# Per-head modulation product moved to GpSimd and VectorE block turns of k and v, in a fused DeltaNet, attention and FFN layer

## The reference, cut to what matters

```python
m = silu(cond) @ w_ada + b_ada        # -> shift1, scale1, gate1, shift2, scale2, gate2
h = rmsnorm(x) * (1 + scale1) + shift1
u = h @ w_in                          # q,k,v,z of 8 DeltaNet heads, betas, attention q,k,v, gates
# A: per head (8 heads, width 128): short conv + silu on q,k,v, l2norm, chunked gated delta
#    rule forward and backward:  v_new = T^-1 (v*beta) - w S ;  o = q S + A v_new ;
#    S = S*gl + (k*decay)^T v_new
# B: neighbourhood attention
x = x + gate1 * ((sig(gA) * (oA @ w_pa) + sig(gB) * (oB @ w_pb)) @ w_out)
x = x + gate2 * swiglu(rmsnorm(x) * (1 + scale2) + shift2)
```

## Time and profile before

| | us |
|---|---|
| median of three runs | 1302.97 (1302.94 to 1303.77) |
| profiled execution | 1302.37 |
| its span, first to last instruction | 1300.6 |

### The profile page before, as it was taken

How to read it: one execution, slowest core, us unless ns; L and a number is a source line. 1 busy time by engine, 2 the same in 40 slices (tenths; PEclk the granted TensorE clock), 3 DMA queues, 4 the chain that set the end, 5 groups by cost and what they waited for, 6 DMA issues and landing times.

```text
span 1300.6 us, 26090 instructions
## 1 busy us (share of the span) xinstructions
PE 1284.3 (99%) x9814; PEld 1212.4 (93%) x9814; DVE 962.6 (74%) x2396; ACT 701.2 (54%) x1578; POOL 172.8 (13%) x161
## 2 busy tenths in 40 slices
PE   7999999999999999999999999999999999999998
PEld 6898999999999999999988889999999999999998
DVE  6677867667686867767456666668999698987995
ACT  5564746465564746465366664347564355634643
POOL 1002020202001020200302320000103300041022
PEclk9999999999999999999999999999999999999999
DMA  9743543434243334325335216431323323233313
GB/s 313 242 131 96 166 122 100 118 94 118 55 142 90 116 103 120 89 72 153 115 113 169 77 51 207 124 82 33 98 67 97 98 70 93 66 100 96 83 57 106
DMA packets 207715, 144.51 MB, mean 111 GB/s; under 512 B 9455, under 2 KB 197015, under 8 KB 207463
## 3 DMA queue, kind: packets, MB, share of 16 engines
q1 hardware_dynamic: 207303, 142.72, 37.4%
q10 hardware_dynamic: 288, 0.13, 0.0%
HBM read 126.67 MB, written 17.99 MB: 111 GB/s over the span
## 4 chain that ended last, share of the span: by engine, by line
PE 92%; DVE 3%; SPq 2%; ACT 1%; issue 1%; DMA 1%; DVEq 0%; ACTq 0%
PE ps L1311 32%; PE ps L1957 25%; PE ps L1700 7%; PE ps L1615 3%; PE ps L1841 2%; PE ps L1937 2%; PE ps L1553 2%; PE ps L1622 2%; SPq L931 2%; PE ps L1439 1%; PE ps L1634 1%; PE ps L1809 1%; PE ps L1285 1%; PE ps L1795 1%; PE ps L1916 1%; PE ps L1693 1%
## 5 line engine op out<-in xcount | busy, mean ns | idle before, releaser
L1311 PE MATMUL ps<-hT_r,WAH_r 128*128 128x320 f32 x624 | 154.9, 329 | 0.5
L1311 PE MATMUL ps<-xT_r,WAH_r 128*128 128x320 f32 x624 | 142.0, 309 | 0.0
L1957 PE MATMUL ps<-d_part_r,W_r 128*128 128x320 f32 x660 | 136.7, 310 | 1.1 <-DVE xT L3388 0.7
L1311 PE MATMUL ps<-hT_r,W_r 128*128 128x320 f32 x588 | 132.6, 308 | 0.0
L1311 PEld LDWEIGHTS ps<-hT_r,WAH_r 128*128 128x128 f32 x624 | 100.3, 189 | 10.8 <-issue 9.8
L1957 PEld LDWEIGHTS ps<-d_part_r,W_r 128*128 128x128 f32 x660 | 107.5, 188 | 2.0 <-DVE xT L3388 1.3
L1957 PE MATMUL ps<-t_big_r,W_r 128*128 128x320 f32 x380 | 107.6, 311 | 0.7 <-ACT naT L2576 0.4
L1311 PEld LDWEIGHTS ps<-xT_r,WAH_r 128*128 128x128 f32 x624 | 104.5, 188 | 0.0
L1957 PE MATMUL ps<-b_part,W_r 128*128 128x320 f32 x456 | 101.2, 309 | 0.0
L1311 PEld LDWEIGHTS ps<-hT_r,W_r 128*128 128x128 f32 x588 | 97.9, 188 | 0.1
L1957 PE MATMUL ps<-t_small_r,W_r 128*128 128x320 f32 x304 | 93.9, 309 | 0.0
(11 more groups left out here) (489 smaller groups left out, 3426.7 us busy)
## 6 DMA issues: line engine op xcount, KB each, us to landing
oT<-in_ffn_w SPq DMA_DIRECT2D x44, 512.0 KB, 5.2
W<-in_w_in SPq DMA_DIRECT2D x36, 512.0 KB, 4.5
WAH<-in_w_ada SPq DMA_DIRECT2D x16, 1024.0 KB, 7.1
naT<-in_w_in SPq DMA_DIRECT2D x24, 512.0 KB, 4.2
ext_dram<-naT SPq DMA_DIRECT2D x28, 320.0 KB, 4.2
oT<-in_ffn_w SPq DMA_DIRECT2D x32, 256.0 KB, 3.9
tA<-ext_dram SPq DMA_DIRECT2D x16, 320.0 KB, 3.7
GCB<-gc_dram SPq DMA_DIRECT2D x7, 640.0 KB, 4.6
```

Of the source, the lines that this page charges most:

```text
L1311: m = e.matmul(ps[:, bank + b, 0:n], w[:, k, :], x[:, k, a:a + n], start=k == 0 and i == 0, stop=k == KD - 1 and i == 2, skip_group_check= ...
L1957: m = e.matmul(ps[:, bank, 0:HT], w[i][:, k, :], x[i][:, k, :], start=start and k == 0 and j == 0, stop=k == half - 1 and j == 2, skip_gro ...
```

## The change

Modulation product. GpSimd now multiplies each 256-column block of `WA` with one column of the condition vectors (`times`, two `tensor_scalar` per block, one for each condition), and adds the eight blocks (`plus`). That is 16 `tensor_scalar` of 128x256 and 7 `tensor_tensor` of 128x512 for each half. The first half stands ahead of "A" in GpSimd's list, the second behind `decays`. TensorE only adds over the partitions: four matmuls of 256 columns (`ada_of_head`) near the end of the head. The loads of `WA` now wait for GpSimd's last `plus` of the half before.

k and v. VectorE turns the 32x32 blocks of k and v in place of TensorE (three block transposes behind "XT3"). SyncE writes the result to DRAM in eight DMAs and reads it back in two, with the blocks in their places, into `kT` and `vrow` (`turns`, behind `ada_second` and the k strip's load). ScalarE makes `kd` from `kT`, now behind "hi 4" and ahead of the "P5 wide" copy. VectorE scales `vrow` in place behind "XT diag". TensorE's list has no turns, and the number of dense steps ahead of some products of the first and middle heads changes by one.

```diff
@@ steps
-    names = ["turn k v"]
-        names += [f"P{n} wide"] + (["ada half"] if n == 4 else []) + ...
+        names += [f"P{n} wide", f"P{n}", f"Y{n} wide", f"Y{n}"]
-POOL_STEPS = ["A", "dt"]
+POOL_STEPS = ada_names(0) + ["A", "dt"] + ada_names(1)
...
@@ SyncE
-                e.wait_ge(pe_dn.sem, pe_dn.value(h - 1, "ada rows"))
+                e.wait_ge(pool_dn.sem, pool_dn.value(h - 1, "plus 1 7"))
                 e.dma_start(WA, w_ada[:, :, ds((16 + h * 4) * P, 2 * P)]).then_inc(ld_wa[0], 16)
             def ada_second(h):
-                e.wait_ge(pe_dn.sem, pe_dn.value(h, "ada half"))
+                e.wait_ge(pool_dn.sem, pool_dn.value(h, "plus 0 7"))
...
+            def turns(h):
+                for w in range(2):
+                    e.wait_ge(dve_dn.sem, dve_dn.value(h, f"{'kv'[w]} turned"))
+                    for a in range(4):
+                        e.dma_start(kv_dram[w][a, :, :, :].rearrange("j q x -> q j x"), turned[w][:, a * (TOK // 4):(a + 1) * (TOK // 4)]).then_inc(st_mid, 16)
+                e.wait_ge(st_mid, 32 + 128 * (h + 1))
+                for w in range(2):
+                    e.dma_start((kT, vrow)[w][:, :], kv_dram[w][:, :, :, :].rearrange("a j q x -> (a j) (q x)")).then_inc(ld_mid, 16)
...
                 if strips_after_next:
                     strip_in("k", h + 2)
+                turns(h)
                 extra_in(h, 2)
                 extra_store(h, 1)
-                rows_out(h)
...
@@ TensorE
-                    "first": (12, 0, 3, 1, 1, 1, 1, 0, 2, 1, 1, 1),
-                    "mid": (12, 2, 2, 2, 2, 2, 2, 1, 3, 2, 1, 1),
+                    "first": (12, 1, 2, 1, 1, 1, 1, 1, 1, 1, 1, 1),
+                    "mid": (12, 2, 2, 2, 2, 2, 2, 2, 2, 2, 1, 1),
-                        m = e.transpose(dst, src, IDN)
-                pe_dn.done(m, "turn k v")
-                        pe_dn.done(ada_rows(4, 2 * P, WA, ld_wa[0:1], h * 16 + 16), "ada half")
-                        pe_dn.done(ada_rows(4, 2 * P, WA, ld_wa[1:2], h * 16 + 16), "ada rows")
+                def ada_of_head():
+                    wait(pool_dn, "plus 1 7")
+                    wait(act_dn, f"v {NT - 1} b")
+                    for j in range(4):
+                        m = e.matmul(ps[32 * j:32 * j + 32, 4, 0:PAIR], ONES[:, 0:32], ada_sums[:, j % 2, j // 2, :], ...)
+                    m.then_inc(mods_mm, 1)
...
@@ ScalarE, behind "hi 4", ahead of the "P5 wide" copy
+                e.wait_ge(ld_mid, 16 * 7 + 32 * h + 32)
+                for u in range(U):
+                    m = e.activation(kd[:, u, :].rearrange("p (q c) -> p q c", q=4), by_quarter[0][:, :, u % NT, :], ACT.Copy, scale=prm[:, EK, u:u + 1])
+                act_dn.done(m, "kd")
...
@@ VectorE
-                done(e.tensor_tensor(vrow[:, 0:CT, :], ps[:, 3, :]..., vb, ALU.mult), "v rows")
-                done(e.tensor_scalar(vrow[:, CT, :], ps[:, 4, P:2 * P], nrm[:, 0, CT:CT + 1], None, ALU.mult), "v ctx")
...
                 turn_x(3)
+                wait(act_dn, "silu v", h - 1)
+                done(e.transpose(to_k, kq[:, :, 0, :]...), "k turned")
+                e.transpose(to_v[:, 0:CT, :, :], conv[:, 2, 1:1 + LAT]...)
+                done(e.transpose(to_v[:, CT, :, :], conv[:, 2, 2 + LAT:2 + TOK]...), "v turned")
...
                 done(m, "XT diag")
+                e.wait_ge(ld_mid, 16 * 7 + 32 * h + 32)
+                done(e.tensor_tensor(by_quarter[1], by_quarter[1], vb, ALU.mult), "v rows")
...
@@ GpSimd
+            def ada_half(h, half):
+                e.wait_ge(ld_wa[half], h * 16 + 16)
+                total = ada_sums[:, half, :, :]
+                def times(k):
+                    out = ada_parts[:, k % 3, :, :] if k else total
+                    for v in range(2):
+                        m = e.tensor_scalar(out[:, v, :], WA[:, k, :], csT[:, k, v:v + 1], None, ALU.mult)
+                    pool_dn.done(m, f"times {half} {k}")
+                times(0)
+                times(1)
+                for k in range(1, KD):
+                    if k + 1 < KD:
+                        times(k + 1)
+                    pool_dn.done(e.tensor_tensor(total, total, ada_parts[:, k % 3, :, :], ALU.add), f"plus {half} {k}")
...
+                ada_half(h, 0)
                 wait(dve_dn, "X3")
...
+                ada_half(h, 1)
```

More of the change, by code:

```diff
@@ L164, in dve_steps @@
 def dve_steps():
-    names = ["L", "L32", "X one", "L32 turned", "L own", "L16", "L16 turned"] + [f"row {t}" for t in range(15)] + ["lo 1", "v rows", "v ctx"]
+    names = ["L", "L32", "X one", "L32 turned", "L own", "L16", "L16 turned"] + [f"row {t}" for t in range(15)] + ["lo 1"]
     for t in range(15):
         names += [f"term {t}", f"lane {t}"] + {6: ["lo 2"], 9: ["lo 2 late"]}.get(t, [])
-    names += ["X3", "XT3", "P4", "lo 3", "X4", "XT4", "lo 4"]
-    names += ["X64", "XT diag", "Y5", "XT64", "lo 5", "P6", "lo z", "Y6", "taps"]
+    names += ["X3", "XT3", "k turned", "v turned", "P4", "lo 3", "X4", "XT4", "lo 4"]
+    names += ["X64", "XT diag", "v rows", "Y5", "XT64", "lo 5", "P6", "lo z", "Y6", "taps"]
     for s in range(NT):
@@ L1091, in _ @@
             ada_second(last)
+            turns(last)
             last_strip(2)
@@ L1115, in _ @@
             pa_in(1)
+            rows_out(last)
             e.wait_ge(st_e, 16 * (NE * (H - 1) + NE_LAST - 1) + 16)
@@ L1504, in sums_free @@
                     elif kind == order[2]:
-                        wait(act_dn, "kd")
-                        wait(dve_dn, "v ctx")
+                        if part == "first":
+                            e.wait_ge(raw["q"], 2)
+                        else:
+                            e.wait_ge(e_out, h * NE + 1)
                     else:
@@ L1651, in head @@
                         norm_rows()
+                        ada_of_head()
+                    if not more and k == 0:
+                        ada_of_head()
                     if not more and k == KD // 2:
@@ L2234, in head @@
                 act_dn.done(m, "L pairs")
-                wait(pe_dn, "turn k v")
-                wait(dve_dn, "v ctx")
-                for u in range(U):
-                    t = u % NT
-                    src = ps[:, 2, t * P:(t + 1) * P] if t < CT else ps[:, 4, 0:P]
-                    m = e.activation(kd[:, u, :], src, ACT.Copy, scale=prm[:, EK, u:u + 1])
-                act_dn.done(m, "kd")
                 if more:
@@ L2997, in conv_next @@
                         if more and name == "v0":
-                            wait(pe_dn, "turn k v")
+                            wait(dve_dn, "v turned")
                         elif more and name[1:] == "0":
```

129 lines of the change are left out of this document (73 added, 56 removed).

## The result

The changed kernel takes 1466.51 us in the median (1464.49 to 1468.38, 4 runs), the kernel before 1303.37 (1302.94 to 1304.15, 4 runs on the same chip): a ratio of 1.125, 95% interval 1.123 to 1.127. It is 163 us slower. The forecast was 1399 with a range of 1328 to 1448: the sign was right, the time lies 67 us above it and 18 above the range.

What follows compares the result with a forecast made beforehand. The prediction took TensorE's list as the bound (busy 99% of the span). Its terms, -16 + 64 + 3 + 45 = +96 us on the profiled 1302.4, gave 1398, forecast as a median of 1399 us, range 1328 to 1448.

Steps and rivals of the forecast that it cites:

- What leaves TensorE's list: TensorE's heads: transposes -0.86, two modulation halves -1.72, `ada_of_head` +0.6; balance -2.0 us a head, -16 for eight.
- Where the first half runs: Beside VectorE's chain L to X3: GpSimd's sums and products hold VectorE, about 8 us late at X3, 64 for eight heads.
- Second half: Modulation's second half on GpSimd behind `decays`, beside VectorE work with some slack: +0.4 us a head, 3 us in all.
- What the bounce costs: At turn P5 TensorE waits for stores, loads, kd and copy: 5.8 us a middle head, 45 in all (30 to 60).
- Rival 3, the clock: Stalls twice a head lower TensorE's clock for the dense steps behind them: 28 us more, 1427; chance 0.17.
- The sum: Whole kernel: -16 + 64 + 3 + 45 = +96 us, giving 1399 us.
- Rivals 1 and 2: 1: only the bounce costs, at turn P5, 1331, chance 0.13; 2: only GpSimd costs, at X3, 1353, chance 0.08.
- 4 and 5: 4: faster, TensorE's list stays the bound, 1286, chance 0.06; 5: costs and savings cancel, 1302, chance 0.02.

Runs made afterwards that it cites:

- e11: Kernel of e2 with GpSimd's sums cut to one column in all heads, the products kept; 1310.16 us, ratio 1.005.
- e1: Changed kernel with the modulation product back on TensorE, k and v still turned by VectorE and bounced through memory; 1413.20 us, ratio 1.084.
- e8: Kernel of e7 with VectorE's "lo 1" issued behind "row 7" instead of "row 14"; 1321.69 us, ratio 1.014.
- e10: Kernel of e2 with GpSimd's products cut to one column in all heads but the first, the sums kept; 1368.29 us, ratio 1.049.
- e3: Kernel of e2 with the first modulation half back on TensorE, only the second on GpSimd behind "A"; 1314.77 us, ratio 1.008.
- e7: Kernel of e1 with kd and "v rows" moved back in their engines' lists, the transfer unchanged; 1327.87 us, ratio 1.019.
- e9: Kernel of e8 with k bounced ahead of v, kd moved in the first head, the last head's loads behind `extra_store(last, 2)`; 1309.71 us, ratio 1.004.
- e12: Kernel of e9 with one whole-row store each for k and v, rearranged in the loads, four kd instructions later, "v rows" split; 1299.97 us, ratio 0.9974.
- e4: Changed kernel with unread matmuls added in all heads but the first, 12 ahead of "P4 wide", 60 ahead of turn P5; 1459.93 us, ratio 1.119.
- e5: Kernel of e1 with 60 unread matmuls added ahead of turn P5 in all heads; 1408.00 us, ratio 1.080.
- e2: Changed kernel with k and v turned by TensorE again, the modulation product still on GpSimd; 1371.09 us, ratio 1.051.

## Why the prediction was wrong

**"What leaves TensorE's list", -2.0 a head.** Modulation: -0.88 at P4 and -0.72 at P6 (e11 against before), 1.60 for the 1.72 forecast. `ada_of_head` costs 0.43 for 0.6. The transposes: -0.86 forecast; e1 shows 0, since "lo 1" is the next thing late at this place, and e8 shows 0.82 once it is not. In the changed kernel this hardly matters, as VectorE's chain is the bound there.

**"Where the first half runs", +8 a head at X3.** Measured: L to X3 longer by 7.1 us, with "v rows" and "v ctx" (0.86) gone from it, so 8.0 of delay. The mechanism was right and the size too, the size partly by luck. A product takes 1.02 us, not 0.4, beyond my upper end of 0.65; that would have ruined the term had products held VectorE. But e11 shows that 16 of them cost the chain 1.4 us (1.4 / 16 = 0.09 each, forecast 0.2), and e10 gives the sums 5.6 us at X3. Second half: forecast 0.4 a head, 0.1 to 0.2 in the changed kernel, where VectorE has slack after the stall; 1.1 in e3, where it has none. The Trainium skill (GPSIMD Engine Reference, Key points) speaks of contention with VectorE's instructions in a 2-port mode or with two SBUF inputs. The trace agrees for those with two inputs where GpSimd runs a sum (1.33 us for 0.3). A copy took 1.23 us for 0.25 as well; in which mode it ran, no run shows.

**"What the bounce costs", +45. This step failed.** The wait, its place and its releaser were as forecast; the terms of its sum were too small. All waits ahead of turn P5 come to 87.5 us. In the middle heads the turn is 11.2 us later in the mean for the 5.8 forecast: 12.1 in the five heads that have the k strip's load ahead of the stores, 6.4 in the sixth, which has none. In these five, from the first store's issue on (means):

- Until all eight stores have landed I had 4.9 us (244.6 to 249.5) and it took 11.7. Of this the issues are 6.5 us, at 0.60 us for one of k's and 0.85 for one of v's (medians of 32) where I had 0.42. Another 5.2 us pass behind the last issue, where I had taken a state store's 1.9 us, counted from its issue's start.
- The two loads took 3.7 us for my 4.6.
- kd and the copy took 3.5 us for my 3.2 (kd alone 3.03 for 2.7).

Together that is 6.2 us more, and it is what was missed: 12.1 for 5.8. My upper end of 8 had issues at 0.6, which alone give 7.2, and so left 0.8 us for "busy queues"; it kept the landing of a lone 64 KB store for the last of eight with 128 rows of 640 bytes each. The first head was worse, 16.9 us for 6.7. There the stores start 4.4 us behind "P4 wide" for my 2.8, right behind two weight loads, and their issues take 9.7 us. The last has 6.5 for 3.2. Why the landing takes so long stays open.

The more useful lesson is in what I asked of the step. I priced the transfer and took kd's place in ScalarE's list as given. e7 shows that the places of the two readers carry 85 of e1's 109 us with the transfer as slow as it is. The other 25 are its length, and with e9 and e12 they go too.

**Rival 3, the clock.** Its mechanism is there, beside the forecast's and not instead of it. It was right on its place (the first steps behind each stall) and on its size: against e11, which has the same TensorE list in these stretches at full clock, P4 wide to turn P4 is 1.43 us longer and turn P5 to P6 1.97, 3.4 us a head, 27 in all; I had 28. I gave it 0.17 as a case of its own, while my forecast had stalls twice a head, longer than any of before. A consequence of the forecast should have stood in its sum. e4 and e5 add that less than this comes back when TensorE is kept busy (6.6 and 5.2 us).

**The sum.** A middle head: 7.0 (X3) - 1.6 (modulation) + 0.4 (`ada_of_head`) + 0.2 (scan and Y6) + 11.2 (P5) + 3.4 (clock) = 20.6, as in the table. Six of them are 123.4; the first head is 24.3 longer and the last, to the end, 17.8, with 0.5 ahead of them 166.0 = 1466.6 - 1300.6. Forecast and result differ by 67: about 42 from the bounce (87.5 for 45) and about 27 from the clock; the small terms give 2 back.

**Rivals 1 and 2** are out, as each part costs by itself (e1, e2); so are 4 and 5.

## What to carry to other kernels

Ask where the result of a detour is read, not only how long it takes: before a reader is given a new source, look whether something else that the bound engine awaits stands behind it in its list, and move the reader first. Count the stores of a rearrangement, and take the landing of the last of a series from a series, not from a lone store. Work given to GpSimd beside a VectorE chain without slack cost here by its two-input instructions, not by its busy time; and if a forecast has new stalls of TensorE, the slower clock behind them belongs in its sum.

## What the runs showed of the hardware

- A one-input GpSimd product of 128x256 took 1.02 us (mean of 224; 0.92 at the least disturbed), near the 1.30 us of a two-input sum of 512 columns and nearly three times a write of 320; with one column it still took 0.36 (mean of 196, e10).
- A sum of GpSimd held the next of many VectorE operations for about 1.05 us: two-input 1.33, copy of 128x160 1.23, one-input 1.28. The 1024-column operations with rounded output took 1.72 to 1.83 where they started under a sum (six in e10), 1.22 where they ran free; three sums of the changed kernel that started under such an operation took 1.8 to 2.2 for 1.3. Not held were block transposes (0.50), the shuffles, copies of 32x160 (0.31, twenty in e10), and operations that read PSUM (r 0.34, S 0.35, in e2 and e10).
- The issue of one DMA on SyncE's queue took 0.34 and 0.43 us for the loads of 320 KB. The 80 KB stores into rows of 640 bytes took 0.60 (k) and 0.85 (v) in the median of the changed kernel, 1.80 at the worst, and 0.5 to 0.6 (one 0.8) in its last two heads, where no strip's load stands right ahead of them.
- TensorE's granted clock fell to the 1.2 GHz level behind an idle of 11.3 us and stood there for 5 us (0.73 over the window to P6). In e5, behind 60 products and an idle of 3.45 us it stayed at 1.00; behind 60 products and one of 3.00 us it fell to 0.50 nine tenths of a microsecond after TensorE had gone on.
- One thing stays open: why SyncE goes on only 5.7 to 6.5 us after it has begun the last store of 640-byte rows (the changed kernel, middle heads), and 3.8 to 5.7 after v's store of 2560-byte rows (e12), where a 64 KB state store takes 1.9.
